# Unread matmuls between TensorE's steps at both ends of a lane-parallel recurrence

## The chip, the cores and the metric

One core of a Trainium2 chip runs the whole program. The metric is the device time of one execution in microseconds. TensorE (PE) does the matmuls, VectorE (DVE), ScalarE (ACT) and GpSimd (POOL) work on their results. A difference of about 0.2%, 6 us here, is what a measurement of this kernel can tell from no change.

## The reference

Two blocks of a language model run one after the other. The first begins with an RWKV-7 time mix over 528 tokens (16 meta tokens and 512 of the sequence), 16 heads of 64. The part in question is its recurrence, once for each head:

```python
def step(S, inp):
    r_t, w_t, k_t, v_t, a_t, b_t = inp
    sa = jnp.einsum('bhij,bhj->bhi', S, a_t)
    S = (S * w_t[:, :, None, :] + sa[..., None] * b_t[:, :, None, :]
         + v_t[..., None] * k_t[:, :, None, :])
    return S, jnp.einsum('bhij,bhj->bhi', S, r_t)
...
_, y = lax.scan(step, S0, seq)
y = jnp.moveaxis(y, 0, 1)
...
return (y * g) @ w_o, v_first
```

Everything after it (norm, gate, output matrix, a convolutional feed-forward network, attention, and the second block with ten times the work) is the same in both kernels.

## The kernel before

The recurrence is not run token by token. The 528 tokens are cut into chunks c = 0 to 3 of 128 tokens and a last chunk c = 4 of 16, and inside a chunk the recurrence is solved with matmuls: a triangular inverse is built by doubling. Two heads make a block (`blk`, 0 to 7), which the code also calls a lane, and two lanes make a couple (`pr`, 0 to 3). A couple goes through a fixed list of steps for each chunk (`lane_steps`): `g0` and `g1` (products within the chunk, the states' decay folded in), `x1`, then `W` and `X` by turns for each level of the doubling (six levels in a chunk of 128, three in the last), then `s1`, `s2`, `s3` and `y`. That makes 19 steps for each of the first four chunks and 13 for the last, 89 in all.

Each step is a few matmuls on PE, followed by the copy or the masking of their result out of PSUM on another engine (`scan_act`, `scan_dve`, `scan_pool`), which the couple's next step waits for. `g0` to `x1` hang on DVE (masks) and POOL, `W` to `X` on a DVE multiplication by a mask, `X` to the next `W` on an ACT copy, `y` to the next chunk's `g0` on POOL and DVE (the new state St).

The order is written out by hand in `SCAN`: in round t, couple p does its step t - 5p (`SKEW` is 5). So couple 0 is alone in rounds 0 to 4, couples 0 and 1 in rounds 5 to 9, three in rounds 10 to 14, four in rounds 15 to 88, then couples 1 to 3 in rounds 89 to 93, couples 2 and 3 in 94 to 98, and couple 3 alone in 99 to 103. All engines follow this one order, and PE executes its steps strictly in it. Each couple has its own two banks of PSUM (bank number = lane number).

Ahead of the recurrence stand the projections (`proj_pe`, line 912) with small sums of line 891; the first `g0` waits for DVE's copy of these sums (`p_sb`, line 1161). Behind it stands `gate_pe`: pairs of `mean(k)` (line 1463) and `squares(k)` (line 1472), which wait for the last `c_ye`, ACT's copy of the last `y`. On ACT and DVE the first work behind the recurrence is the split of a weight chunk (line 296, then 303), and only then DVE's centring of the first piece (line 1559) and ACT's squares (line 1540).

`ident` and `ones` are constants of 128 x 128 in f32, in the tile `cst`. The PE helper lines in the recurrence: 1269 (`g0`, `g1`), 1280, 1283 and 1286 (`x1`), 1295 (`W`), 1302 and 1305 (`X`), 1313 (`s1`), 1319 (`s2`), 1326 to 1329 (`s3`), 1335 to 1350 (`y`). In the profile an f32 matmul has two records for one in the program, an f16 one has one.

Of the kernel before, what the change touches and what calls it, by code (L numbers as in the profile page):

```python
# [7 lines left out]
F32 = mybir.dt.float32  # L8
# [230 lines left out]
def program(nc, d_h, d_ctx, d_vec, d_cst, d_csr, d_csb, d_csw, d_slc, d_w, d_ada, d_cond, d_out):  # L239
    with ExitStack() as ctx:  # L240
# [10 lines left out]
        psum = ctx.enter_context(nc.psum_tensor("psum", [128, 8, 512], F32))  # L251
# [6 lines left out]
        ident = cst[:, CST["ident"]:CST["ident"] + 128]  # L258
        ones = cst[:, CST["ones"]:CST["ones"] + 128]
# [402 lines left out]
        RA = mem.left("RA", [128, 2, 8, L])  # L662
# [4 lines left out]
        KT = mem.left("KT", [128, 8, L])  # L667
# [17 lines left out]
        BT = mem.left("BT", [128, 8, L])  # L685
        vtok = mem.left("vtok", [128, 5, D])
# [13 lines left out]
        v_out = more(r_out, [(j, b) for j in range(4) for b in range(3)])  # L700
# [21 lines left out]
        p_sb = sig("p_sb", [(ti,) for ti in range(5)])  # L722
# [451 lines left out]
        IH = mem.left("IH", [128, 128], F16)  # L1174
# [15 lines left out]
        def lane_steps(c):  # L1190
            n = 7 if c < 4 else 4
            out = ["g0", "g1", "x1"]
            for lvl in range(1, n):
# [5 lines left out]
        _steps = [(c, s) for c in range(5) for s in lane_steps(c)]  # L1199
        SCAN = [(p, *_steps[_t - SKEW * p]) for _t in range(len(_steps) + 3 * SKEW) for p in range(4)  # L1200
                if 0 <= _t - SKEW * p < len(_steps)]
        ONES = [(blk, c, s) for p, c, s in SCAN for blk in (2 * p, 2 * p + 1)]
        at = lambda name: [(blk, c) for blk, c, s in ONES if s == name]
        lvls = lambda name: [(blk, c, s[1] if s[0] == "X" else 0) for blk, c, s in ONES if s[0] == name or (name == "X" and s == "x1")]
# [45 lines left out]
        mUI = csr[:, CSR["mUI"]:CSR["mUI"] + 128]  # L1250
        lvT0 = csr[:, CSR["lvT0"]:CSR["lvT0"] + 128]

        def scan_pe(e):
            for pr, c, s in SCAN:
                two = [Lane(blk, c) for blk in (2 * pr, 2 * pr + 1)]
                if s in ("g0", "g1"):
                    w = int(s[1])
                    if w:
                        e.wait_ge(*c_gm.at(two[1].blk, c, 0, 1))
                    elif c:  # L1260
                        e.wait_ge(*c_S.at(two[1].blk, c - 1, 1))
                    else:
                        e.wait_ge(*p_sb.at(4))
                        e.wait_ge(*p_op.at("r", two[1].blk))
                        e.wait_ge(*v_out.at(3, 2))
                    for l, q in enumerate(two):
                        for j in range(2):
                            rows = slice(64 * j, 64 * j + 64)
                            ins = e.matmul(q.pg[:, j, l, :, 0:q.T], (BT, KT)[w][rows, q.blk, q.tok], RA[rows, :, q.blk, q.tok],  # L1269
                                           start=True, stop=True)  # L1270
                    ins.then_inc(*c_g.up(pr, c, w))
                    continue
                for q in two:
                    blk, T = q.blk, q.T
                    if s == "x1":
                        e.wait_ge(*c_ai.at(blk, c, 1))
                        e.wait_ge(*c_gm.at(two[1].blk, c, 1, 1))
                        e.wait_ge(*c_I.at(1))
                        for j in range(2):
                            e.matmul(q.px[:, j, 0:T], q.Xh[0:T, 2 + j, 0:T], IH[0:T, 0:T], start=True, stop=True)  # L1280
                        if not c:
                            e.wait_ge(*c_S0.at(blk))
                        e.matmul(q.p[:, 256:384], RA[:, 0, blk, q.tok], q.S[:, :], start=True, stop=False, skip_group_check=True)
                        for j in range(2):
                            h = 2 * blk + j
                            ins = e.matmul(q.p[:, 256 + 64 * j:320 + 64 * j], q.Ak[0:T, j, 0:T], vtok[0:T, c, 64 * h:64 * h + 64],  # L1286
                                           start=False, stop=True, skip_group_check=True)
                        ins.then_inc(*c_x.up(blk, c, 0))
                    elif s[0] == "W":
                        e.wait_ge(*c_xe.at(blk, c, s[1] - 1))  # L1290
                        if s[1] == 1:
                            e.wait_ge(*c_ar.at(blk, c))
                            e.wait_ge(*c_z1e.at(blk, c))
                        for j in range(2):
                            ins = e.matmul(q.px[:, j, 0:T], q.Ah[0:T, j, 0:T], q.Xh[0:T, j, 0:T], start=True, stop=True)
                        ins.then_inc(*c_w.up(blk, c, s[1]))
                    elif s[0] == "X":
                        e.wait_ge(*c_we.at(blk, c, s[1]))
                        f = True
                        for j in range(2):  # L1300
                            if s[1] < q.NL - 1:
                                e.matmul(q.px[:, j, 0:T], q.Xh[0:T, 2 + j, 0:T], q.Wh[0:T, j, 0:T], start=f, stop=False,
                                         skip_group_check=True)
                                f = False
                            ins = e.matmul(q.px[:, 2 + j, 0:T], q.Wh[0:T, j, 0:T], q.Xh[0:T, 2 + j, 0:T], start=f, stop=True,  # L1305
                                           skip_group_check=True)
                            f = False
                        ins.then_inc(*c_x.up(blk, c, s[1]))
                    elif s == "s1":
                        e.wait_ge(*c_xe.at(blk, c, q.NL - 1))  # L1310
                        e.wait_ge(*c_zr.at(blk, c))
                        for j in range(2):
                            ins = e.matmul(q.p[:, 64 * j:64 * j + 64], q.X[0:T, j, 0:T], q.Zr[0:T, 64 * j:64 * j + 64],
                                           start=True, stop=True)
                        ins.then_inc(*c_s1.up(blk, c))
                    elif s == "s2":
                        e.wait_ge(*c_s1e.at(blk, c))
                        for j in range(2):
                            ins = e.matmul(q.p[:, 128 + 64 * j:192 + 64 * j], q.A[0:T, j, 0:T], q.Wr[0:T, 0, 64 * j:64 * j + 64].bitcast(F32),  # L1319
                                           start=True, stop=True)  # L1320
                        ins.then_inc(*c_s2.up(blk, c))
                    elif s == "s3":
                        e.wait_ge(*c_s2e.at(blk, c))
                        if c < 4:
                            for w, src in enumerate((BT, KT)):
                                e.transpose(q.p[:, 128 + 128 * w:256 + 128 * w], src[:, blk, q.tok], ident)
                        e.matmul(q.p[:, 0:128], II[0:T, 0:T], q.Wr[0:T, 0, :], start=True, stop=False, skip_group_check=True)
                        for j in range(2):
                            ins = e.matmul(q.p[:, 64 * j:64 * j + 64], q.X[0:T, j, 0:T], q.Wr[0:T, 1, 64 * j:64 * j + 64],
                                           start=False, stop=True, skip_group_check=True)  # L1330
                        ins.then_inc(*c_s3.up(blk, c))
                    elif s == "y":
                        y, st = q.pf[:, 128:128 + T], q.pf[:, 256:320]
                        e.wait_ge(*c_u.at(blk, c))
                        e.matmul(y, q.S[:, :], RA[:, 1, blk, q.tok], start=True, stop=False, skip_group_check=True)
                        for j in range(2):
                            h = 2 * blk + j
                            e.matmul(y[64 * j:64 * j + 64, :], vtok[0:T, c, 64 * h:64 * h + 64], q.R[0:T, 2 + j, 0:T],
                                     start=False, stop=False, skip_group_check=True)
                        if c < 4:  # L1340
                            for j in range(2):
                                h = 2 * blk + j
                                e.matmul(st[64 * j:64 * j + 64, :], q.tB[0:T, 1, 64 * j:64 * j + 64], vtok[0:T, c, 64 * h:64 * h + 64],
                                         start=False, stop=False, skip_group_check=True)
                        for j in range(2):
                            ins = e.matmul(y[64 * j:64 * j + 64, :], q.U[0:T, 64 * j:64 * j + 64], q.R[0:T, j, 0:T],
                                           start=False, stop=True, skip_group_check=True)
                        if c < 4:
                            for j in range(2):
                                ins = e.matmul(st[64 * j:64 * j + 64, :], q.tB[0:T, 0, 64 * j:64 * j + 64], q.U[0:T, 64 * j:64 * j + 64],  # L1350
                                               start=False, stop=True, skip_group_check=True)
                        ins.then_inc(*c_y.up(blk, c))

        def scan_act(e):
            e.wait_ge(*p_sb.at(4))
# [1825 lines left out]
```

## Time and profile before

| | us |
|---|---|
| median of 3 runs | 2995.22 |
| lowest, highest | 2992.68, 2999.0 |
| the profiled execution | 2993.15 |
| its span, first to last instruction | 2991.4 |
| the recurrence in it (first g0 to the gate's first matmul) | 276.9 |

The profile page divides the span into 40 slices of 75 us. The recurrence fills from the end of slice 4 to the end of slice 7. Views of single stretches give for each the busy time of every engine and the TensorE clock granted there (1.00 is 2.4 GHz, 0.50 is 1.2 GHz). Start times of PE are those of the first of a group of records; since matmuls are pipelined and their ends are modelled, the cost of one is better read from the distance between starts, or from the chain of waits, than from a record's duration.

### The profile page before, as it was taken

To read this page: it belongs to the slowest core of one execution; us is meant where nothing else is said; L and a number is where in the kernel's file an instruction comes from. 1 tells how busy PE (TensorE), PEld (TensorE's weight loads), DVE (VectorE), ACT (ScalarE), POOL (GpSimd) and SP (SyncE) were. 2 spreads that over 40 slices of the span, in tenths; PEclk is the share of its full clock that TensorE was granted. 3 is DMA by queue.
4 is the path that set the end of the run, shared out by engine and by line. 5 is a ranking of instruction groups with operands and counts; after the bars stand their busy time and mean duration, and the time that the engine had idled before them with its cause. 6 is when DMAs were issued, how large, how long until landed. Compare 5 with 4: busy or idle time off the path is not lost.

```text
span 2991.4 us, 46812 instructions
## 1 busy us (share of the span) xinstructions
PE 2913.9 (97%) x19658; PEld 2583.3 (86%) x19658; DVE 1797.0 (60%) x2666; ACT 1300.3 (43%) x2153; POOL 483.1 (16%) x405
## 2 busy tenths in 40 slices
PE   6998999999999999999999999999999999999999
PEld 6997887899999999999999977667888878788887
DVE  7776664579597453547949757655535543465453
ACT  4575664344243455644424445654323332343231
POOL 0002221123032000002303313001202111121020
PEclk9998997999999999999999999999999999999999
DMA  2210000245554321025545520102232222223232
GB/s 103 89 53 36 2 2 6 75 156 183 170 170 164 113 88 36 1 79 183 176 164 189 188 99 29 43 17 83 94 97 88 97 90 93 91 85 101 90 97 86
DMA packets 79554, 284.34 MB, mean 95 GB/s; under 512 B 8528, under 2 KB 9296, under 8 KB 78576
## 3 DMA queue, kind: packets, MB, share of 16 engines
q1 hardware_dynamic: 79344, 281.35, 28.1%
q8 instruction: 155, 2.54, 0.3%
q14 instruction: 55, 0.45, 0.0%
HBM read 274.96 MB, written 6.36 MB: 94 GB/s over the span
## 4 chain that ended last, share of the span: by engine, by line
PE 93%; DVE 4%; ACT 2%; issue 1%; POOL 1%; DMA 0%; SPq 0%; DVEq 0%; ACTq 0%
PE psum L348 67%; PE psum L2733 2%; PE psum L1893 2%; PE psum L912 2%; PE psum L2104 2%; PE psum L2086 1%; PE psum L2077 1%; PE psum L1269 1%; PE psum L848 1%; PE psum L539 1%; PE psum L1319 1%; PE psum L1286 1%; PE psum L2430 1%; PE psum L2727 1%; PE psum L2721 1%
## 5 line engine op out<-in xcount | busy, mean ns | idle before, releaser
L303 DVE TENSOR_TENSOR wlo<-wraw,whi 128x1024 fp32r<-128x1024 f32 (+2 forms) x398 | 507.7, 1297 | 614.7 <-ACT whi L296 605.8
L296 ACT CAST whi<-wraw 128x1024 fp32r<-128x1024 f32 (+2 forms) x398 | 396.3, 1021 | 495.2 <-PE psum L348 460.6
L431 DVE CUSTOM_DVE_ANT_0 araw<-araw,cond 128x1024 f32<-128x1024 f32 x112 | 181.1, 1654 | 0.0
L348 PE MATMUL psum<-f0xh,whi 128*128 128x264 f32 x704 | 143.1, 285 | 0.0
L348 PE MATMUL psum<-f0xh,wlo 128*128 128x264 f32 x704 | 143.0, 285 | 0.0
L348 PE MATMUL psum<-f0xl,whi 128*128 128x264 f32 x704 | 142.4, 284 | 0.0
L348 PE MATMUL psum<-f1xh,whi 128*128 128x258 f32 x704 | 141.9, 283 | 0.0
L348 PE MATMUL psum<-f1xh,wlo 128*128 128x258 f32 x704 | 141.9, 283 | 0.0
L348 PE MATMUL psum<-f1xl,whi 128*128 128x258 f32 x704 | 141.4, 282 | 0.0
L348 PE MATMUL psum<-f2xh,whi 128*128 128x512 f32 x352 | 139.1, 395 | 1.0 <-DVE f2xl L592 1.0
L348 PE MATMUL psum<-f3xh,whi 128*128 128x512 f32 x352 | 139.1, 395 | 1.0 <-DVE f3xl L592 1.0
L348 PE MATMUL psum<-f2xh,wlo 128*128 128x512 f32 x352 | 139.0, 395 | 0.0
L348 PE MATMUL psum<-f3xh,wlo 128*128 128x512 f32 x352 | 139.0, 395 | 0.0
L348 PE MATMUL psum<-f2xl,whi 128*128 128x512 f32 x352 | 139.0, 395 | 0.0
L348 PE MATMUL psum<-f3xl,whi 128*128 128x512 f32 x352 | 139.0, 395 | 0.0
L348 PEld LDWEIGHTS psum<-f0xh,whi 128*128 128x128 f32 x704 | 109.3, 189 | 0.1
L348 PEld LDWEIGHTS psum<-f1xh,wlo 128*128 128x128 f32 x704 | 109.2, 190 | 0.0
L348 PEld LDWEIGHTS psum<-f1xh,whi 128*128 128x128 f32 x704 | 109.1, 189 | 0.1
L348 PEld LDWEIGHTS psum<-f0xh,wlo 128*128 128x128 f32 x704 | 109.1, 189 | 0.0
L348 PEld LDWEIGHTS psum<-f1xl,whi 128*128 128x128 f32 x704 | 109.0, 189 | 0.0
L348 PEld LDWEIGHTS psum<-f0xl,whi 128*128 128x128 f32 x704 | 108.8, 188 | 0.0
L1371 ACT ACTIVATE XH<-psum 128x512 f16<-128x512 f32 (+1 forms) x176 | 88.6, 562 | 25.1 <-PE psum L1305 24.9
(515 smaller groups left out, 8193.9 us busy)
## 6 DMA issues: line engine op xcount, KB each, us to landing
wraw<-d_w SPq DMA_DIRECT2D x357, 512.0 KB, 3.4
araw<-d_ada SPq DMA_DIRECT2D x112, 512.0 KB, 3.3
wraw<-d_w SPq DMA_DIRECT2D x32, 384.0 KB, 3.6
hn<-d_h SPq DMA_DIRECT2D x4, 528.0 KB, 7.9
hres<-d_h SPq DMA_DIRECT2D x1, 2112.0 KB, 8.2
spill<-hres SPq DMA_DIRECT2D x1, 2112.0 KB, 7.4
hres<-spill SPq DMA_DIRECT2D x1, 2112.0 KB, 8.5
cond<-d_cond SPq DMA_DIRECT2D x2, 1024.0 KB, 4.8
```

The source lines that it names most:

```text
L296: e.copy(whi[0:rows, n % NH, 0:kt * cols], wraw[0:rows, n % NR, 0:kt * cols]).then_inc(*w_hi.up(n))
L303: e.tensor_tensor(wlo[0:rows, n % NH, 0:kt * cols], wraw[0:rows, n % NR, 0:kt * cols], whi[0:rows, n % NH, 0:kt * cols].bitcast(F32), ALU. ...
L348: ins = e.matmul(psum[0:bw, b0 + nb * len(sl) + si, 0:ln], l_ if z == 2 else h_, (xp.lo if z == 1 else xp.hi)[:, k, o:o + ln], start=k == ...
L431: e.tensor_tensor_reduce(out=w, in0=w, in1=self.c[:, col, :], scale=1.0, scalar=0.0, op0=ALU.mult, op1=ALU.add, accum_out=ada[:, ly, blk, ...
L539: ins = e.matmul(rms_psum(ntok, bank, h), ones, sq[:, i, h * half:(h + 1) * half], start=i == 0, stop=i == 2)
L848: ins = e.matmul(psum[:, key_bank(j) + 2 * nb + si, 0:ln], (wl if z == 2 else wh)[:, i, 128 * nb:128 * nb + 128], (xs.lo if z == 1 else xs ...
L912: ins = e.matmul(psum[0:ln, b, 256 * (ti % 2):256 * (ti % 2) + 256], a_, w_[:, i, :], start=k == 0 and z == 0 and ti % 2 == 0, stop=k == 7 ...
L1269: ins = e.matmul(q.pg[:, j, l, :, 0:q.T], (BT, KT)[w][rows, q.blk, q.tok], RA[rows, :, q.blk, q.tok], start=True, stop=True)
L1371: e.activation(to, q.px[:, o:4, 0:T], ACT.Copy).then_inc(*c_xe.up(blk, c, s[1]))
L1893: ins = e.matmul(psum[0:ln, b, 256 * (ti % 2):256 * (ti % 2) + 256], a_, w_[:, k - k0, :], start=k == 0 and z == 0 and ti % 2 == 0, stop=k ...
L2104: ins = e.matmul(psum[:, 6 + half, lo_ - a0:hi_ - a0], vz, wtt[:, w % 2, col + lo_ - a:col + hi_ - a], start=kb == 2 and hh % 2 == 0, stop ...
L2733: ins = e.matmul(psum[:, b, :], vw[:, ts_[q][0], kv, :], Pw[:, n % NP, :], start=q == 0, stop=q == NQ[g] - 1, skip_group_check=True)
```

## The change

Between PE's steps the kernel now issues matmuls whose result nobody reads, in the rounds in which fewer than four couples are under way. The function `unread` issues 2 x (4 - active) f32 matmuls of `ident` (stationary) with `ones` (moving, 128 columns), each complete in itself, after the last couple's step of the round: 6 a round while one couple is there, 4 with two, 2 with three. `LAST_IN` holds, for the last step of each round, the number of couples done and the number under way. While couples are still to start, the results go to bank 7 of PSUM, that of the last lane. When couples are done, they go to bank 0, and PE waits first for ACT's copy of couple 0's last `y` (`c_ye` of lane 1), whose bank it was. The rounds are 0 to 14 and 89 to 103: 5 x (6 + 4 + 2) = 60 matmuls on each side, 120 in all. Nothing else is changed: the body of `scan_pe` became `scan_step` and lost an indentation, so that line numbers behind it are 17 higher.

```diff
+        LAST_IN = {}
+        for _t in range(len(_steps) + 3 * SKEW):
+            there = [p for p in range(4) if 0 <= _t - SKEW * p < len(_steps)]
+            LAST_IN[(there[-1], *_steps[_t - SKEW * there[-1]])] = (there[0], len(there))
...
+        def unread(e, done, active):
+
+            if done:
+                e.wait_ge(*c_ye.at(1, 4))
+            for _ in range(2 * (4 - active)):
+                e.matmul(psum[:, 0 if done else 7, 0:128], ident, ones, start=True, stop=True)
+
         def scan_pe(e):
             for pr, c, s in SCAN:
-                two = [Lane(blk, c) for blk in (2 * pr, 2 * pr + 1)]
...
+                scan_step(e, pr, c, s)
+                done, active = LAST_IN.get((pr, c, s), (0, 4))
+                if active < 4:
+                    unread(e, done, active)
+
+        def scan_step(e, pr, c, s):
+            two = [Lane(blk, c) for blk in (2 * pr, 2 * pr + 1)]
...
```

PE's order at the start of the recurrence, rounds 0 to 3 (couple 0: g0, g1, x1, W). Line 891 is the last of the projections; before:

```order
L891 MATMUL psum<-cst,kqr 16x2
L1269 MATMUL psum<-RA,BT 128x256 x4
L1269 MATMUL psum<-RA,KT 128x256 x4
L1280 MATMUL psum<-IH,XH 128x128 x2
L1283 MATMUL psum<-St,RA 128x128
L1286 MATMUL psum<-vtok,AK 128x64 x2
L1280 MATMUL psum<-IH,XH 128x128 x2
L1283 MATMUL psum<-St,RA 128x128
L1286 MATMUL psum<-vtok,AK 128x64 x2
L1295 MATMUL psum<-XH,AH 128x128 x4
L1302 MATMUL psum<-WH,XH 128x128
```

The same place in the changed kernel (lines 17 higher; the unread matmuls are those of line 1262):

```order
L891 MATMUL psum<-cst,kqr 16x2
L1286 MATMUL psum<-RA,BT 128x256 x4
L1262 MATMUL psum<-cst 128x128 x6
L1286 MATMUL psum<-RA,KT 128x256 x4
L1262 MATMUL psum<-cst 128x128 x6
L1297 MATMUL psum<-IH,XH 128x128 x2
L1300 MATMUL psum<-St,RA 128x128
L1303 MATMUL psum<-vtok,AK 128x64 x2
L1297 MATMUL psum<-IH,XH 128x128 x2
L1300 MATMUL psum<-St,RA 128x128
L1303 MATMUL psum<-vtok,AK 128x64 x2
L1262 MATMUL psum<-cst 128x128 x6
```

No step has changed its place; six matmuls stand in front of each of the next steps.

PE's order at the end, rounds 99 to 103 (couple 3 alone, chunk of 16 tokens: X, s1, s2, s3, y) and the gate's first matmul; before:

```order
L1305 MATMUL psum<-XH,WH 16x16 x4
L1313 MATMUL psum<-Zr,XT 16x64 x4
L1319 MATMUL psum<-WR,ZA 16x64 x4
L1327 MATMUL psum<-WR,II 16x128
...
L1329 MATMUL psum<-WR,XT 16x64 x2
L1335 MATMUL psum<-RA,St 128x16
...
L1346 MATMUL psum<-RBK,ZA 64x16 x2
L1463 MATMUL psum<-RA,cst 128x264 x4
```

The same place in the changed kernel:

```order
L1322 MATMUL psum<-XH,WH 16x16 x4
L1262 MATMUL psum<-cst 128x128 x6
L1330 MATMUL psum<-Zr,XT 16x64 x4
L1262 MATMUL psum<-cst 128x128 x6
L1336 MATMUL psum<-WR,ZA 16x64 x4
L1262 MATMUL psum<-cst 128x128 x6
L1344 MATMUL psum<-WR,II 16x128
...
L1346 MATMUL psum<-WR,XT 16x64 x2
L1262 MATMUL psum<-cst 128x128 x6
...
L1363 MATMUL psum<-RBK,ZA 64x16 x2
L1262 MATMUL psum<-cst 128x128 x6
L1480 MATMUL psum<-RA,cst 128x264 x4
```

Here too the steps stand as before, with six matmuls ahead of s1, s2, s3 and y, and six more between the last y and the gate's first matmul.

## Rows read from the trace of the kernel before

**Rows 1.** The page: share of each engine, then the granted clock in 40 slices
```profile
PE 2913.9 (97%) x19658; PEld 2583.3 (86%) x19658; DVE 1797.0 (60%) x2666; ACT 1300.3 (43%) x2153; POOL 483.1 (16%) x405
PEclk9998997999999999999999999999999999999999
```

**Rows 2.** Busy time by stretch of 1 us: start of the recurrence
```profile
core 0: us, PE busy (x) PEld busy (x) DVE busy (x) ACT busy (x) POOL busy (x), PEclk, DMA share, GB/s
244.00:245.00 1.00, 0.54 (x2) 0.50 (x4) 0.40 (x5) 0.50 (x2) 0.00 (x0) 0.59 0.99 401
...
261.00:262.00 1.00, 0.36 (x5) 0.14 (x4) 0.80 (x4) 1.00 (x3) 0.92 (x2) 0.88 0.00 0
...
268.00:269.00 1.00, 0.87 (x11) 0.53 (x9) 0.50 (x2) 1.00 (x4) 0.00 (x0) 0.97 0.00 0
```

**Rows 3.** The same view at the end of the recurrence and behind it
```profile
489.00:490.00 1.00, 1.00 (x15) 0.95 (x14) 0.29 (x3) 0.70 (x4) 0.25 (x1) 0.97 0.00 0
490.00:491.00 1.00, 1.00 (x16) 0.92 (x16) 0.00 (x0) 0.19 (x2) 0.00 (x0) 0.50 0.00 0
...
527.00:528.00 1.00, 1.00 (x5) 0.83 (x4) 0.13 (x1) 0.00 (x0) 0.00 (x0) 0.76 0.96 414
```

**Rows 4.** PE in order of time: start, length, line, tiles, idle before
```profile
244.46 2.08 PE L1269 MATMUL psum<-RA,BT 64*128 64x256 f32 x8 [0.58 <-DVE sbt L1161]
248.14 2.08 PE L1269 MATMUL psum<-RA,KT 64*128 64x256 f32 x8 [1.60 <-DVE RBK L1397]
...
251.95 0.74 PE L1283 MATMUL psum<-St,RA 128*128 128x128 f32 x2
252.48 0.95 PE L1286 MATMUL psum<-vtok,AK 128*128 128x64 f32 x4
...
257.15 0.40 PE L1295 MATMUL psum<-XH,AH 128*128 128x128 f16 x2
```

**Rows 5.** The same, in rounds 10 to 16 of the start, at full clock
```profile
276.61 0.27 PE L1280 MATMUL psum<-IH,XH 128*128 128x128 f16 x2 [0.79 <-POOL XH L1422]
...
278.17 0.39 PE L1295 MATMUL psum<-XH,AH 128*128 128x128 f16 x4
...
280.50 0.61 PE L1313 MATMUL psum<-Zr,XT 128*128 128x64 f32 x4
...
287.55 0.44 PE L1283 MATMUL psum<-St,RA 128*128 128x128 f32 x2
287.82 0.56 PE L1286 MATMUL psum<-vtok,AK 128*128 128x64 f32 x4
```

**Rows 6.** The same, at the end: last full-clock y of 16 tokens, then rounds 90 on
```profile
489.17 0.38 PE L1335 MATMUL psum<-RA,St 128*128 128x16 f32 x2
...
489.81 0.52 PE L1335 MATMUL psum<-RA,St 128*128 128x16 f32 x2
...
497.47 0.39 PE L1313 MATMUL psum<-Zr,XT 16*16 16x64 f32 x4
...
503.95 0.40 PE L1269 MATMUL psum<-RA,BT 64*16 64x32 f32 x8 [0.35 <-DVE St L1412]
...
509.86 0.29 PE L1305 MATMUL psum<-XH,WH 16*16 16x16 f16 x4
...
516.00 0.43 PE L1305 MATMUL psum<-XH,WH 16*16 16x16 f16 x4 [0.22 <-DVE WH L1401]
```

**Rows 7.** The chain of waits through the last y and the gate's start
```profile
518.91 0.54 PE psum L1335 x2
...
521.36 3.89 PE psum L1463 x8
...
528.24 0.89 PE psum L1472 x4
```

**Rows 8.** DVE in order of time behind the last y
```profile
522.27 1.23 DVE L303 TENSOR_TENSOR wlo<-wraw,whi 128x1024 fp32r<-128x1024 f32 x1 [3.81 <-ACT whi L296]
523.53 0.71 DVE L1559 SCALAR_TENSOR_TENSOR RA<-psum,RA 128x528 f32<-128x528 f32 x1
```

More of the change, by code:

```diff
@@ L1251, in program @@
         lvT0 = csr[:, CSR["lvT0"]:CSR["lvT0"] + 128]
+        def unread(e, done, active):
[3 more added lines that the diff above has]
+                e.matmul(psum[:, 0 if done else 7, 0:128], ident, ones, start=True, stop=True)
         def scan_pe(e):
             for pr, c, s in SCAN:
-                two = [Lane(blk, c) for blk in (2 * pr, 2 * pr + 1)]
[L1256 to L1283, printed above, removed]
+                scan_step(e, pr, c, s)
@@ new lines, in scan_pe @@
+                done, active = LAST_IN.get((pr, c, s), (0, 4))
[3 more added lines that the diff above has]
+            two = [Lane(blk, c) for blk in (2 * pr, 2 * pr + 1)]
+            if s in ("g0", "g1"):
+                w = int(s[1])
+                if w:
+                    e.wait_ge(*c_gm.at(two[1].blk, c, 0, 1))
+                elif c:
+                    e.wait_ge(*c_S.at(two[1].blk, c - 1, 1))
+                else:
+                    e.wait_ge(*p_sb.at(4))
+                    e.wait_ge(*p_op.at("r", two[1].blk))
+                    e.wait_ge(*v_out.at(3, 2))
+                for l, q in enumerate(two):
+                    for j in range(2):
+                        rows = slice(64 * j, 64 * j + 64)
+                        ins = e.matmul(q.pg[:, j, l, :, 0:q.T], (BT, KT)[w][rows, q.blk, q.tok], RA[rows, :, q.blk, q.tok],
+                                       start=True, stop=True)
+                ins.then_inc(*c_g.up(pr, c, w))
+                return
+            for q in two:
+                blk, T = q.blk, q.T
+                if s == "x1":
+                    e.wait_ge(*c_ai.at(blk, c, 1))
+                    e.wait_ge(*c_gm.at(two[1].blk, c, 1, 1))
+                    e.wait_ge(*c_I.at(1))
+                    for j in range(2):
+                        e.matmul(q.px[:, j, 0:T], q.Xh[0:T, 2 + j, 0:T], IH[0:T, 0:T], start=True, stop=True)
+                    if not c:
+                        e.wait_ge(*c_S0.at(blk))
+                    e.matmul(q.p[:, 256:384], RA[:, 0, blk, q.tok], q.S[:, :], start=True, stop=False, skip_group_check=True)
+                    for j in range(2):
+                        h = 2 * blk + j
+                        ins = e.matmul(q.p[:, 256 + 64 * j:320 + 64 * j], q.Ak[0:T, j, 0:T], vtok[0:T, c, 64 * h:64 * h + 64],
+                                       start=False, stop=True, skip_group_check=True)
+                    ins.then_inc(*c_x.up(blk, c, 0))
+                elif s[0] == "W":
+                    e.wait_ge(*c_xe.at(blk, c, s[1] - 1))
+                    if s[1] == 1:
+                        e.wait_ge(*c_ar.at(blk, c))
+                        e.wait_ge(*c_z1e.at(blk, c))
+                    for j in range(2):
+                        ins = e.matmul(q.px[:, j, 0:T], q.Ah[0:T, j, 0:T], q.Xh[0:T, j, 0:T], start=True, stop=True)
+                    ins.then_inc(*c_w.up(blk, c, s[1]))
+                elif s[0] == "X":
+                    e.wait_ge(*c_we.at(blk, c, s[1]))
+                    f = True
+                    for j in range(2):
+                        if s[1] < q.NL - 1:
+                            e.matmul(q.px[:, j, 0:T], q.Xh[0:T, 2 + j, 0:T], q.Wh[0:T, j, 0:T], start=f, stop=False,
+                                     skip_group_check=True)
+                            f = False
+                        ins = e.matmul(q.px[:, 2 + j, 0:T], q.Wh[0:T, j, 0:T], q.Xh[0:T, 2 + j, 0:T], start=f, stop=True,
+                                       skip_group_check=True)
+                        f = False
+                    ins.then_inc(*c_x.up(blk, c, s[1]))
+                elif s == "s1":
+                    e.wait_ge(*c_xe.at(blk, c, q.NL - 1))
+                    e.wait_ge(*c_zr.at(blk, c))
+                    for j in range(2):
+                        ins = e.matmul(q.p[:, 64 * j:64 * j + 64], q.X[0:T, j, 0:T], q.Zr[0:T, 64 * j:64 * j + 64],
+                                       start=True, stop=True)
+                    ins.then_inc(*c_s1.up(blk, c))
+                elif s == "s2":
+                    e.wait_ge(*c_s1e.at(blk, c))
+                    for j in range(2):
+                        ins = e.matmul(q.p[:, 128 + 64 * j:192 + 64 * j], q.A[0:T, j, 0:T], q.Wr[0:T, 0, 64 * j:64 * j + 64].bitcast(F32),
+                                       start=True, stop=True)
+                    ins.then_inc(*c_s2.up(blk, c))
+                elif s == "s3":
+                    e.wait_ge(*c_s2e.at(blk, c))
+                    if c < 4:
+                        for w, src in enumerate((BT, KT)):
+                            e.transpose(q.p[:, 128 + 128 * w:256 + 128 * w], src[:, blk, q.tok], ident)
+                    e.matmul(q.p[:, 0:128], II[0:T, 0:T], q.Wr[0:T, 0, :], start=True, stop=False, skip_group_check=True)
+                    for j in range(2):
+                        ins = e.matmul(q.p[:, 64 * j:64 * j + 64], q.X[0:T, j, 0:T], q.Wr[0:T, 1, 64 * j:64 * j + 64],
+                                       start=False, stop=True, skip_group_check=True)
+                    ins.then_inc(*c_s3.up(blk, c))
+                elif s == "y":
+                    y, st = q.pf[:, 128:128 + T], q.pf[:, 256:320]
+                    e.wait_ge(*c_u.at(blk, c))
+                    e.matmul(y, q.S[:, :], RA[:, 1, blk, q.tok], start=True, stop=False, skip_group_check=True)
+                    for j in range(2):
+                        h = 2 * blk + j
+                        e.matmul(y[64 * j:64 * j + 64, :], vtok[0:T, c, 64 * h:64 * h + 64], q.R[0:T, 2 + j, 0:T],
+                                 start=False, stop=False, skip_group_check=True)
+                    if c < 4:
@@ L1284, in scan_pe @@
                         for j in range(2):
                             h = 2 * blk + j
-                            ins = e.matmul(q.p[:, 256 + 64 * j:320 + 64 * j], q.Ak[0:T, j, 0:T], vtok[0:T, c, 64 * h:64 * h + 64],
-                                           start=False, stop=True, skip_group_check=True)
[L1288 to L1352, printed above, removed]
@@ new lines, in scan_step @@
+                            e.matmul(st[64 * j:64 * j + 64, :], q.tB[0:T, 1, 64 * j:64 * j + 64], vtok[0:T, c, 64 * h:64 * h + 64],
+                                     start=False, stop=False, skip_group_check=True)
+                    for j in range(2):
+                        ins = e.matmul(y[64 * j:64 * j + 64, :], q.U[0:T, 64 * j:64 * j + 64], q.R[0:T, j, 0:T],
+                                       start=False, stop=True, skip_group_check=True)
+                    if c < 4:
+                        for j in range(2):
+                            ins = e.matmul(st[64 * j:64 * j + 64, :], q.tB[0:T, 0, 64 * j:64 * j + 64], q.U[0:T, 64 * j:64 * j + 64],
+                                           start=False, stop=True, skip_group_check=True)
@@ L1354, in scan_act @@
+                    ins.then_inc(*c_y.up(blk, c))
         def scan_act(e):
```

## The prediction

> **What bounds the kernel now.** I read the page first: PE is busy for 97% of the span and no other engine for more than 60% [rows 1], so anything added on PE has a price unless it falls into one of PE's gaps. The granted clock by slices is 0.9 or more but for two slices, the fourth with an 8 and the seventh with a 7 [rows 1]. Both touch an end of the recurrence, and that is where the change adds its matmuls, so the next view is the busy time by stretches of 1 us there. At the start the clock falls to its half level (1.2 GHz) at about 244.2, is full (2.4 GHz) from 261.1 for some 3.5 us, half again and full for good from 268.0 [rows 2]. Before the fall PE had done sums of two columns each for 2 us; before the rises it had been busy without a gap. At the end the clock falls at 489.97 and comes back only at 527.5, after six microseconds of the gate's long matmuls [rows 3]. So two stretches of 20 and 37.5 us run at half the clock, and these are all that the unread matmuls could win back. How much of such a stretch is tied to the clock differs: a step waits for DVE, ACT or POOL as often as for PE at the start [rows 4], and hardly at the end, where PE shows no gap over 0.4 us [rows 6].
>
> **What one unread matmul costs.** The nearest row is line 1283, one f32 matmul of 128 columns: its two records and the next line's start are 0.53 us apart at half clock (251.95 to 252.48) and 0.27 at full (287.55 to 287.82) [rows 4, 5]. A lower bound comes from long matmuls standing back to back, where loading weights is wholly hidden: four records of 264 columns in 0.89 us at full clock, eight in 3.89 at half [rows 7]; by columns that is 2 x 0.2225 x 128/264 = 0.22 us and 2 x 0.486 x 128/264 = 0.47. Unread matmuls stand in runs of 2 to 6, between the two kinds, so I take 0.24 and 0.48. A run of six is 1.44 or 2.88 us, of four 0.96 or 1.92, of two 0.48 or 0.96. All 120 together are 28.8 us at full clock, 57.6 at half, before anything is hidden.
> The Trainium skill ("TensorE: Matmul & The Clock Gate", "Step-by-step: what each phase is for") says that the engine pulls the loading of weights ahead of matmuls in flight; by it the lower bound would hold, and the sum would be up to 120 x 0.02 = 2.4 us smaller. Line 1283 costs more than that in this trace, but between matmuls of other types.
>
> **The start, rounds 0 to 14** (244.46 to 280.50, 36.0 us). PE's order is strict, so a run of unread matmuls delays the next step by what exceeds the gap there.
> Rounds 0 to 4: before, 12.7 us (244.46 to 257.15) [rows 4]. Round 0 begins at half clock: g0 2.08 and six unread 2.88 are 4.96 against 3.68, +1.3. PE has then no gap from 244.46 on, and I expect the full clock during round 0 or round 1. Round 1: g1 takes 1.1 to 2.1, and DVE's masks behind it (as the idle of 1.60 behind g0 [rows 4]) cover the six: 2.6 to 3.6 against 3.64. Round 2: x1 at full clock is 1.56 (276.61 to 278.17 [rows 5]), with six 3.0, against 2.94. Rounds 3 and 4, W and X of one couple: 0.25 and 0.43 of work at full clock and 1.44 each, 3.6 against 2.43. Sum 14.2 to 15.2, that is +1.5 to +2.5.
> Rounds 5 to 9 (257.15 to 269.84, 12.7 us): at full clock throughout 2.3 + 2.7 + 3.1 + 1.65 + 1.65 = 11.4, since g0, g1 and x1 halve and rounds 6 and 7 have waits for DVE under which the four unread lie: -1.3.
> Rounds 10 to 12 wait for masks too (0.79 us ahead of 276.61, and two like it), which covers 0.48: +0.1. Rounds 13 and 14 (278.17 to 280.50 [rows 5]) have no gap: +1.0.
> Start: **+1.8**, between 0 (0.22 each, clock back at once) and +3.5 (0.27, clock back in round 2).
>
> **Rounds 15 to 88** hold no added instruction; they start later and last as long. The clock's fall at 489.97 lies in round 88, while the first unread matmul of the end stands behind round 89's s3 (497.4). So the fall stays, and the first 7.4 us at half clock too. The wait for c_ye of lane 1 costs nothing: that y was finished at 490.8, and behind the wait only work of round 90 is queued.
>
> **The end, rounds 89 to 103 and the gate.** Work of T = 16 costs 0.6 at full clock of what it costs at half: the first lane's y is 0.64 us (489.17 to 489.81 [rows 6]), and 1.09 at half (the last y's first lane, 518.91 to 520.00, [rows 7] for its start).
> Rounds 89 to 93 (to 509.86): 5 x 0.96 = 4.8 at half clock, less 0.35 of the gap ahead of 503.95 [rows 6] and 0.15 of smaller ones: +4.3. Two in each round leave most of the time to matmuls of 16 rows or columns, under which the clock was not given back in 30 us although PE shows as busy, so I leave it at half here.
> Rounds 94 to 98 (509.86 to 516.00, 6.1 us [rows 6]): four unread fill two thirds of a round. I let round 94 pass at half (0.85 + 1.92 = 2.8) and the others at full clock: 3.1 of work and 4 x 0.96 = 7.0. Sum 9.8, **+3.6**.
> Rounds 99 to 103: to the last y's end before 5.1 us; after, 2.6 of work at full clock and 4 x 1.44 = 8.4, +3.3. The six behind the last y are hidden: DVE centres the first piece only at 523.53, after ACT's 1.04 and its own 1.23 on a weight chunk [rows 8], 2.4 us after y's end, and six unread plus mean(0) at full clock are 1.44 + 0.89 = 2.3. Behind that the gate gains from the clock what lies between 523.5 and 527.5: sixteen records of which DVE's and ACT's pieces set part, 1.4 us. Together **+1.9**.
> End: 4.3 + 3.6 + 1.9 = **+9.8**.
>
> **Sum.** 1.8 + 9.8 = +11.6 us on the profiled execution's 2993.15: 3004.8, taken as 3005. That execution lies 2.1 us under the median; the runs spread by 6.3, so I add nothing for it. Nothing behind the gate can swallow the shift, since PE is the bound there to the end [rows 1].
>
> **Rivals.**
> (a) The clock comes back early at the end, in round 90: couple 3's y of 128 tokens is 4.4 us of dense f32, followed now by unread ones. Then rounds 89 and 90 add 1.4, rounds 91 to 93 go from 7.4 to 4.6 + 1.4 = 6.0 (-1.4), rounds 94 to 98 need 3.4 + 4.8 = 8.2 (+2.1), and the last part stays +1.9: +4.0, with the start +5.8, 2999. For it: dense f32 preceded the rise at 527.5. Against it: the same y in 498.1 to 502.5 did not bring the clock back. This is **not slower** by my bound, and it decides at the point where the clock is full before 503.
> (b) It doesn't come back until the gate: +4.3; rounds 94 to 98 9.6 less 0.5 of gaps, +9.1; four runs of six 11.5 less 0.4, +11.1; the last run delays mean(0) past 523.5, +1.5. End +26, 3021. For it: PE shows 1.00 busy at half clock for 30 us [rows 3]. Against it: from round 99 on three quarters of PE's time would be full 128 x 128 f32 work. The Trainium skill ("TensorE: Matmul & The Clock Gate", "What's actually happening") says that the throttled state is the default and activity releases it. By it (a) or my forecast would hold rather than (b); the trace agrees at 261 and 527, and shows at 490 that a PE busy in the records isn't enough.
> (c) The start stays at half clock until 261 as before: rounds 0 to 4 then add 1.3 + 1.3 + 2.9 + 2.2 + 2.4 = 10.1, rounds 5 to 14 some 2, so the whole is +22, 3015.
> (d) Faster: the fall at 490 moves behind round 89, because the later start puts other rounds under the clock's look, and unread ones then hold it. That is worth 0.4 x 7.4 = 3 us on top of (a); with the start's best value of 0 the whole is +1 to -1, 2992 to 2994. So even this is no clear gain: 28.8 us of matmuls stand against stretches of 37.5 and 20 us at half clock, of which 0.4 at most, 15 and 8 us, could come back.
>
> **Chances.** My forecast 0.50, (a) 0.24, (b) 0.13, (c) 0.07, (d) 0.06. The range runs from (a) less 1.5 us to (b): 2997.5 to 3021. Measurement can tell 0.2% from no change. Slower by more (over 3001): forecast, (b), (c) and a part of (a), 0.73. Within: most of (a) and (d), 0.24. Faster: 0.03.
>
> **What the changed profile would show.** Half clock for under 8 us from 244, and round 15's s1 near 282; rounds 3 and 4 of 1.7 to 1.9 us, with six unread each; the fall in round 87 to 89 as before; the clock full again around round 95, and y's end to the gate's first matmul 1.5 us apart. I would be wrong in the sum if an unread matmul cost other than 0.22 to 0.27 us at full clock, and in the sign if the clock stayed full from round 88 on.

## The result, and the profile after

The changed kernel takes 3017.90 us (median of four runs, 3014.59 to 3024.2) against 2996.97 for the kernel before (four runs): 21 us more, a ratio of 1.0074 [1.0053, 1.0095]. The profiled execution took 3016.87, its span 3015.0 against 2991.4. Slower, as forecast, by more than the 11.6 us of the sum and inside the range. One execution of the kernel before in a later comparison took 4760 us at a mean granted clock of 0.553; it is left out of every figure here.

The page of the changed kernel: the engines' shares, then the granted clock by slices.

```profile
PE 2945.1 (98%) x19898; PEld 2616.7 (87%) x19898; DVE 1795.9 (60%) x2666; ACT 1300.5 (43%) x2153; POOL 483.7 (16%) x405
...
PEclk9999997999999999999999999999999999999999
```

PE has 240 records more (120 f32 matmuls, two records each) and 31.2 us more of busy time; the other engines are as in [rows 1]. The 8 in the fourth slice has gone, the 7 in the seventh has not. Stretches of 2 us of the changed kernel (columns as in [rows 2]; the last but two is the granted clock):

```profile
474.00:476.00 2.00, 1.66 (x34) 1.23 (x28) 2.00 (x13) 1.30 (x7) 0.70 (x4) 1.00 0.00 0
476.00:478.00 2.00, 2.00 (x22) 1.36 (x22) 0.95 (x9) 1.67 (x5) 0.23 (x1) 0.55 0.03 8
...
490.00:492.00 2.00, 1.39 (x28) 1.06 (x26) 1.15 (x5) 0.28 (x1) 0.60 (x1) 1.00 0.00 0
...
504.00:506.00 2.00, 2.00 (x19) 1.43 (x20) 0.00 (x0) 0.70 (x5) 0.00 (x0) 0.50 0.00 0
...
512.00:514.00 2.00, 2.00 (x38) 1.78 (x37) 0.53 (x5) 0.86 (x6) 0.78 (x4) 1.00 0.00 0
...
518.00:520.00 2.00, 2.00 (x19) 1.65 (x19) 0.00 (x0) 0.59 (x4) 0.00 (x0) 0.50 0.00 0
...
532.00:534.00 2.00, 2.00 (x10) 2.00 (x11) 0.00 (x0) 0.11 (x2) 0.00 (x0) 0.50 0.00 0
534.00:536.00 2.00, 2.00 (x19) 1.82 (x18) 0.00 (x0) 0.42 (x2) 0.00 (x0) 0.94 0.00 0
...
1188.00:1190.00 2.00, 2.00 (x11) 2.00 (x9) 1.46 (x3) 1.49 (x3) 0.00 (x0) 0.50 0.00 0
```

Followed us by us, the clock is at half in 244 to 247.5 (before: 17 + 3.4 us there [rows 2]), in 476 to 490, which the kernel before shows at full clock, in 493 to 510, in 517.2 to 534.2, and later for ten us in the attention (1186 to 1196) and for 3.4 us at 1773. PE in order of time at the two ends; line 1262 is the unread matmuls, 1480 the gate's first:

```profile
244.15 2.08 PE L1286 MATMUL psum<-RA,BT 64*128 64x256 f32 x8 [0.58 <-DVE sbt L1161]
246.16 2.23 PE L1262 MATMUL psum<-cst 128*128 128x128 f32 x12
248.33 1.14 PE L1286 MATMUL psum<-RA,KT 64*128 64x256 f32 x8
249.39 1.60 PE L1262 MATMUL psum<-cst 128*128 128x128 f32 x12
251.03 0.27 PE L1297 MATMUL psum<-IH,XH 128*128 128x128 f16 x2
...
252.59 1.56 PE L1262 MATMUL psum<-cst 128*128 128x128 f32 x12
253.98 0.39 PE L1312 MATMUL psum<-XH,AH 128*128 128x128 f16 x4
...
503.36 1.20 PE L1262 MATMUL psum<-cst 128*128 128x128 f32 x4
504.49 0.39 PE L1330 MATMUL psum<-Zr,XT 16*16 16x64 f32 x4
...
519.69 2.08 PE L1262 MATMUL psum<-cst 128*128 128x128 f32 x8
521.69 1.03 PE L1336 MATMUL psum<-WR,ZA 16*16 16x64 f32 x8
...
531.79 2.75 PE L1262 MATMUL psum<-cst 128*128 128x128 f32 x12
534.48 0.30 PE L1330 MATMUL psum<-Zr,XT 16*16 16x64 f32 x4
534.71 1.60 PE L1262 MATMUL psum<-cst 128*128 128x128 f32 x12
...
541.33 1.60 PE L1262 MATMUL psum<-cst 128*128 128x128 f32 x12
542.77 1.95 PE L1480 MATMUL psum<-RA,cst 128*128 128x264 f32 x8
```

Six cost 1.39 us at full clock (252.59 to 253.98), 0.23 each; four cost 2.0 at half (519.69 to 521.69), 0.50 each. The parts, each from one step's start to another's:

| part | before | after | difference |
|---|---|---|---|
| rounds 0 to 14 (first g0 to couple 0's first s1) | 36.0 | 35.8 | -0.2 |
| rounds 15 to 89 (to the last transpose of s3) | 216.1 | 222.7 | +6.5 |
| from there to the gate's first matmul | 24.7 | 40.1 | +15.4 |
| gate, to its second squares | 6.7 | 4.4 | -2.3 |
| everything behind (+4.5) and ahead (-0.3) | | | +4.2 |

### The profile page after: what moved, and what is told of

It is laid out like the page before. It is cut to its first block, busy times and chain, and to the rows that moved or that the text cites. A ratio compares the mean times of both kernels' runs of the same rounds, so it can differ in the third digit from the quotient of the medians.

```text
span 3015.0 us, 47292 instructions
## 1 busy us (share of the span) xinstructions
PE 2945.1 (98%) x19898; PEld 2616.7 (87%) x19898; DVE 1795.9 (60%) x2666; ACT 1300.5 (43%) x2153; POOL 483.7 (16%) x405
## 4 chain that ended last, share of the span: by engine, by line
PE 93%; DVE 4%; ACT 1%; issue 1%; POOL 0%; DMA 0%; SPq 0%; DVEq 0%; ACTq 0%
PE psum L348 67%; PE psum L2750 2%; PE psum L1910 2%; PE psum L912 2%; PE psum L2121 2%; PE psum L1262 1%; PE psum L2103 1%; PE psum L2094 1%; PE psum L1286 1%; PE psum L848 1%; PE psum L539 1%; PE psum L1336 1%; PE psum L2447 1%; PE psum L2744 1%; PE psum L2738 1%
```

## Experiments

One yardstick for all: the three stretches of the recurrence in one profiled execution, and the ratio to the kernel before where it was timed. "Early stretch" is half clock that begins between 460 and 480 us; it lies ahead of a fall between 485 and 495 that every profile has. "End to gate" begins at the last transpose of round 89.

| kernel | rounds 0-14 | 15-89 | end to gate | early stretch | ratio |
|---|---|---|---|---|---|
| before | 36.0 | 216.1 | 24.7 | no | |
| before, profiled again | 34.7 | 223.6 | 24.7 | 460-477 | |
| the change | 35.8 | 222.7 | 40.1 | 476-490 | 1.0074 [1.0053, 1.0095] |
| start only | 35.8 | 222.7 | 24.7 | 474-488 | 1.0002 [0.9991, 1.0013] |
| end only | 34.7 | 223.6 | 42.8 | 463-480 | 1.0058 [1.0037, 1.0078] |
| 12 behind round 14 | 38.6 | 221.9 | 24.2 | 478-491 | 1.0020 [1.0009, 1.0031] |
| rounds 0 to 2 only | 32.4 | 222.8 | 24.7 | 470-485 | 0.9992 [0.9979, 1.0004] |
| the same, timed again | 32.4 | 222.9 | 24.7 | 473-487 | 0.9985 [0.9974, 0.9996] |
| end only, doubled | 36.5 | 221.3 | 46.5 | 479-489 | |
| end only, f16 | 35.4 | 216.0 | 33.0 | no | |
| f16, both ends | 34.2 | 217.1 | 33.1 | no | 1.0051 [1.0032, 1.0071] |
| hold, f32 | 32.4 | 222.0 | 27.2 | no | 1.0004 [0.9994, 1.0013] |
| hold, f16 | 32.2 | 219.3 | 26.4 | no | 1.0012 [1.0000, 1.0024] |

**Which side costs: start only, end only.** (The words behind # in the edits shown here are notes for the reader.)

```diff
-                if active < 4:
+                if active < 4 and not done:      # start only
+                if active < 4 and done:          # end only
```

> Unread matmuls in rounds 0 to 14 alone (60 of them), none at the end. Theory A (the lost time is the price of unread matmuls at the end; the stretch of half clock at 476 to 489.5 is a matter of where the clock's changes fall, not of the unread matmuls themselves): rounds 0 to 14 take 35.8 us as in the changed kernel, and the whole is within 6 us of the kernel before, on either side. Theory B (the start's matmuls move the recurrence so that the clock falls near 476 each time, which costs some 6.5 us): half clock shows before round 86 again and the kernel is 6 us or more slower than before. The forecast's sum had +1.8 us for the start.

> Unread matmuls in rounds 89 to 103 alone. Theory A: rounds 89 to 103 take 38 to 42 us against 26.2 before, the gate gives back 2, so the kernel is 12 to 15 us slower than before, and the rounds before 89 are as in the kernel before. Theory B: the same end, and the fall of the clock at 490 as before, so 12 to 15 too; start only and end only would then add up to the change's 21. If the clock stays full from round 90 on (the second rival of the prediction), only 4 us slower.

Start only is the same as before (1.0002), end only 17 us slower (1.0058, 11 to 23). So the end's 60 matmuls account for nearly all of the change's loss. End only lost more than the 12 to 15 expected: in its profile the clock was at half again from 514.4 to 538.3. And end only, whose program is the kernel before up to round 89, had the early stretch (462 to 464 at 0.80, 468 at half). So it isn't the start's shift that brings it (theory B): that fell here.

**A shift alone: 12 unread matmuls behind round 14.**

```diff
+                if t == 14:
+                    unread(e, 0, -2)
```

> The kernel before with one run of 12 unread matmuls behind round 14, at full clock: rounds 15 to 103 are the same work, only shifted by 12 x 0.23 = 2.8 us. Theory A: 2.8 us for the run; where the clock falls in rounds 75 to 90 changes with the shift, so the total lies anywhere from 0 to 9 us above before. Theory B, as far as it blames the shift: half clock before round 86 shows here also. If the clock falls in round 88 as in the kernel before, the shift alone doesn't move the fall.

The twelve stand in one run (line 1262), ahead of round 15's s1 (line 1330):

```profile
276.75 0.54 PE L1322 MATMUL psum<-XH,WH 128*128 128x128 f16 x4
...
278.10 2.90 PE L1262 MATMUL psum<-cst 128*128 128x128 f32 x24
280.75 0.61 PE L1330 MATMUL psum<-Zr,XT 128*128 128x64 f32 x4
```

Round 14 with them lasts from 276.75 to 280.75, 4.0 us, where the two profiles of the kernel before have 1.3: 2.7 us for the twelve, as their price says. The whole is 6 us slower (1.0020, 3 to 9). That is more than 2.7 by its median, and its lower end agrees with 2.7; what the rest is, if it is anything, no stretch of this profile shows. The early stretch is there once more, as theory A allows and theory B asks.

**Is the early stretch the kernel's own: before, profiled again.**

> The kernel before, unchanged, profiled once more. In five profiles of kernels with unread matmuls (one of which has none ahead of round 89) the clock fell between 463 and 477, came back for some 3 to 12 us near 481 to 494 and fell again; rounds 15 to 89 took 222 to 224 us there, and 216 in the one profile of the kernel before. Theory A (that stretch comes and goes on its own and was absent from the first profile by chance): half clock shows near 460 to 480 here too, and round 15's s1 to round 89's last transpose takes about 222. Theory B (it comes from the unread matmuls or the new program): it is absent again, 216.

Stretches of the kernel before in this second profile:

```profile
456.00:458.00 2.00, 1.44 (x26) 1.10 (x26) 1.30 (x6) 1.36 (x3) 0.60 (x1) 1.00 0.00 0
...
462.00:464.00 2.00, 2.00 (x15) 1.10 (x13) 0.24 (x1) 0.34 (x2) 0.00 (x0) 0.50 0.03 8
...
468.00:470.00 2.00, 2.00 (x16) 2.00 (x16) 0.00 (x0) 1.04 (x3) 0.00 (x0) 0.50 0.00 0
...
476.00:478.00 2.00, 1.82 (x27) 1.31 (x26) 1.78 (x9) 1.47 (x3) 0.12 (x1) 0.68 0.00 0
...
480.00:482.00 2.00, 2.00 (x21) 1.44 (x21) 0.54 (x5) 1.35 (x6) 0.00 (x0) 1.00 0.03 8
```

The unchanged kernel has it, with 223.6 us for rounds 15 to 89. It comes up in the rounds in which the 16-token chunk's small matmuls begin to replace large ones, and it comes and goes from one execution to another: of the profiles without any addition between rounds 15 and 88, eight have it and three have not (before, f16 end, f16 both ends). So the +6.5 in the table of parts is no cost of the change. The first profile of the kernel before, on which the prediction was built, happened to lack it. The granted clock of whole executions says the same: that profile had 0.987, and of the 64 later runs of the kernel before 46 had 0.982 to 0.985.

**Does the clock follow the number or the kind: doubled, f16.** Both on top of end only.

```diff
-            for _ in range(2 * (4 - active)):
+            for _ in range(4 * (4 - active)):      # doubled
...
+            for _ in range(8 * (4 - active)):      # f16
+                e.matmul(psum[:, 0 if done else 7, 0:128], IH[:, :], IH[:, :], start=True, stop=True)
```

> Unread matmuls at the end alone, twice as many (4, 8 and 12 a round, 120 in all). By price alone at full clock 60 more cost 60 x 0.23 = 13.8 us over the end-only kernel's 42.8 from round 89's last transpose to the gate: 57. Theory C (in rounds 94 to 98 the clock stayed at half because the unread matmuls were too few beside work of 16 columns): with eight a round it is full from round 94 or 95 on, rounds 94 to 98 take 13 us or less in spite of 20 more matmuls (14.8 in the changed kernel), and the whole end is 50 to 52. Theory D (the clock follows something else there): half clock in rounds 94 to 98 again, these alone 25 us, the end 60 or more.

> Unread matmuls at the end alone, in f16 (the f16 identity with itself, 128 columns), four for each f32 one: 8, 16 and 24 a round. One f16 matmul stands 0.055 us from the next at full clock and 0.107 at half in this trace, so four cost 0.22 or 0.43 us, as one f32. Theory C: the end takes as long as with f32, 38 to 43 us, with the clock full or half in much the same rounds. If f16 ones at the same time of PE bring the clock back in rounds 94 to 98 where f32 ones did not, the end takes about 33 to 35: then the kind of matmul matters and not only PE's busy time.

Doubled (rounds 91, then 95 and 96), then f16 (rounds 94 to 98); the unread matmuls are those of line 1262:

```profile
511.71 1.16 PE L1262 MATMUL psum<-cst 128*128 128x128 f32 x8
512.80 0.23 PE L1344 MATMUL psum<-WR,II 16*16 16x128 f32 x1
...
521.26 2.05 PE L1262 MATMUL psum<-cst 128*128 128x128 f32 x16
523.24 0.61 PE L1336 MATMUL psum<-WR,ZA 16*16 16x64 f32 x8
...
523.87 2.05 PE L1262 MATMUL psum<-cst 128*128 128x128 f32 x16
```

```profile
509.27 1.79 PE L1262 MATMUL psum<-IH 128*128 128x128 f16 x16
511.00 0.39 PE L1330 MATMUL psum<-Zr,XT 16*16 16x64 f32 x4
...
511.60 1.63 PE L1262 MATMUL psum<-IH 128*128 128x128 f16 x16
513.16 0.62 PE L1336 MATMUL psum<-WR,ZA 16*16 16x64 f32 x8
...
513.79 1.07 PE L1262 MATMUL psum<-IH 128*128 128x128 f16 x16
...
515.41 1.07 PE L1262 MATMUL psum<-IH 128*128 128x128 f16 x16
```

Eight f32 unread matmuls take 1.98 us at full clock here (521.26 to 523.24), as long as four at half in the changed kernel: twice as many cost nothing more in these rounds, because the clock was full. The doubled end took 46.5 us, 3.7 more than end only, where 60 matmuls at full clock cost 13.8. Both forecasts for the end, 50 to 52 and 60 or more, were too high. Of the two, theory C is the one that this profile bears out: more unread work held the clock. It doesn't say how much is needed in a round. After its rise at 510 the doubled kernel's clock did not fall again in the recurrence, neither in rounds 91 to 93, where four stood beside the matmuls of 16 columns, nor in rounds 94 to 98 with eight. In the changed kernel two a round stood in rounds 91 to 93; the clock fell just behind them, at 517.2, and four a round did not bring it back in 17 us. So four a round held a full clock in one place and didn't restore it in another, and it is one profile of the doubled kernel.

With f16 the clock rose at 503, fell for 3.4 us at 509.5 and was full from 513 on; the end took 33.0. The rise is no earlier in the work than with f32: 7.3 us behind the last transpose, against 7.7 to 8.1 in the profiles of the change, of end only and of the doubled kernel. What differs is the fall behind it, 3.4 us long instead of 17 and 24.

**The change with f16.**

> The change itself with f16 instead of f32, four for one, so that PE's time for them is the same (480 instead of 120). Theory E (f16 matmuls of the same length bring the clock back sooner): the end takes 33 us from round 89's last transpose to the gate, as with the end alone in f16, against 40.2 with f32; with 2.3 back in the gate and 35 to 36 at the start, 5 to 9 us slower than before where the change is 21 slower. Theory C (it was chance that the clock came back early in that one profile): 38 to 43 again, and 15 to 22 us slower than before.

The profile repeats the 33 at the end, but the runs don't repeat the profile: it took 3004.70 at a mean granted clock of 0.991, the other three 3013 to 3017 at 0.986 or 0.987, which is 24 to 30 us more at half clock. The ratio is 1.0051 [1.0032, 1.0071], and overlaps the change's. So the forecast of 5 to 9 us fell for the median. In two profiles out of two the second fall was shorter with f16 than in the two profiles with as much f32. But these are also the two that lack the early stretch, which both f32 ones have, so the kind of matmul isn't the only difference; an advantage over f32 isn't shown.

**What is worth keeping: rounds 0 to 2 alone.**

```diff
+                if 0 <= t < 3:
+                    unread(e, done, active)
```

> Six unread matmuls in each of rounds 0 to 2 only, 18 in all. In the changed kernel rounds 0 to 4 took 13.3 us with 30 unread matmuls, of which those of rounds 0 and 1 lay under masks on DVE and those of rounds 2 to 4 in the open. Theory A: the clock rises at 247.5 as in the changed kernel; if it then stays full without further unread matmuls, rounds 0 to 14 take 33 us or less against 36.0 before, and the kernel is 3 us faster than before, less than its runs spread. If the clock falls again at about 258 to 265, as it did there in the kernel before, the gain is 1 us or nothing.

> The kernel with six f32 unread matmuls in each of rounds 0 to 2 and none elsewhere, measured again with more rounds, since 0.9992 [0.9979, 1.0004] leaves open whether it is faster. Its profile had rounds 0 to 14 at 32.4 us, against 36.0 and 34.6 in the two profiles of the kernel before. If that holds, 2 to 3.6 us faster, a ratio of 0.9988 to 0.9993. If the clock's other changes swamp it, 1.0000.

PE in the second of these profiles:

```profile
246.75 2.14 PE L1262 MATMUL psum<-cst 128*128 128x128 f32 x12
248.82 1.13 PE L1286 MATMUL psum<-RA,KT 64*128 64x256 f32 x8
249.89 1.60 PE L1262 MATMUL psum<-cst 128*128 128x128 f32 x12
251.53 0.27 PE L1297 MATMUL psum<-IH,XH 128*128 128x128 f16 x2
...
253.09 1.56 PE L1262 MATMUL psum<-cst 128*128 128x128 f32 x12
...
257.06 1.13 PE L1286 MATMUL psum<-RA,BT 64*128 64x256 f32 x8
...
259.81 1.14 PE L1286 MATMUL psum<-RA,KT 64*128 64x256 f32 x8 [1.05 <-DVE RBK L1414]
...
262.51 0.27 PE L1297 MATMUL psum<-IH,XH 128*128 128x128 f16 x2 [1.24 <-POOL XH L1439]
```

The six of round 0 and the six of round 1 lie for the most part under the waits for DVE's masks, and g1's records take 1.13 instead of 2.08 [rows 4]: round 1 falls from 3.6 to 2.7 us. The six of round 2 lie in the open, but x1 beside them runs at full clock, and the round takes 2.9 us, as before. Behind them the clock stays full though PE has gaps again; rounds 3 to 14 take 3.2 us less than in the first profile of before and 1.8 less than in the second, which is most of the gain. Rounds 0 to 14 take 32.4 us in both profiles, against 36.0 and 34.7 before. Measured first, the kernel's difference was not clear of zero; measured again, it is 0.9985 [0.9974, 0.9996], some 4.5 us faster than before, anything from 1 to 8. The granted clock agrees: 20 of this kernel's 21 runs had 0.987 or more, of the kernel before's 64 only 11. So it is faster than both kernels, by somewhat less than 0.2%.

**Holding the clock through the last chunk: f32, f16.** Besides rounds 0 to 2, unread matmuls of 112 columns ahead of lane 0's own in couple 0's steps of the last chunk (rounds 76 to 88), and a few in rounds 89 to 93. The second kernel has f16 ones throughout, 24 a round in rounds 0 to 2.

```diff
+        def fill(e, q):
+            if q.blk == 0 and q.c == 4:
+                for _ in range(2):                 # 4, and IH twice, in the f16 kernel
+                    e.matmul(psum[:, 0, 400:512], ident, ones[:, 0:112], start=True, stop=True)
...
+                if 0 <= t < 3 or 89 <= t < 94:
+                    unread(e, done, active)
```

> Candidate. Six unread matmuls in rounds 0 to 2 as in the run of the first three rounds; two of 112 columns in each of couple 0's steps of the last chunk (rounds 76 to 88, ahead of its own matmuls, lane 0 only), two in rounds 89 to 93; none behind. The price at full clock is 18 + 26 to 44 + 10 times some 0.2. If these hold the clock from round 76 on, rounds 15 to 89 take 217 to 220 us instead of 222.8, rounds 89 to 93 about 12 instead of 14.8, and with the start's 2 to 3.6 us the kernel is 5 to 9 us faster than before. If the clock falls near 470 all the same, ahead of or in spite of them, they cost 8 to 15 us at half clock and the kernel is 4 to 12 us slower.

> Candidate with f16 unread matmuls: 24 in each of rounds 0 to 2 (as long as six f32 ones), four of 112 columns in each of couple 0's steps of the last chunk (rounds 76 to 88), four in rounds 89 to 93, none behind. In the hold with f32 ones the early stretch of half clock was absent but they cost 4 us at full clock, so nothing was won. Here the price is 13 x 4 x 0.05 = 2.6 us. If f16 ones hold the clock from 470 to 490 or beyond, rounds 15 to 89 take 218 to 219 us against 216 (no early stretch) and 223 (with it), and the whole is 3 to 7 us faster than before. If the clock falls near 488 as ever and stays down to the gate, 0 to 3 us faster; if it falls early too, 0 to 3 us slower.

Neither had the early stretch, but both fell to half at 486 all the same, the second for 41 us. Rounds 15 to 89 took 222.0 and 219.3 instead of the 216 to 217 of executions without the stretch: most of what the stretch costs went into the matmuls that were to prevent it, and neither the 5 to 9 us hoped for from the first kernel came nor the 0 to 7 from the second. With ratios of 1.0004 and 1.0012 both are 4 to 8 us worse than rounds 0 to 2 alone. Since the stretch also stays away by itself, two profiles don't show that they prevented it.

## Why the prediction was right, point by point

**The sign and its reason held.** PE is the bound, the clock's fall lies ahead of the end's first unread matmul, and their price at the end exceeds what the clock gives back. Start only and end only show this apart: 0 and 17 us.

**The price** of 0.24 and 0.48 a piece was 0.23 and 0.50.

**Start, forecast +1.8**: -0.2 against the profile it was reckoned from, +1.2 against the second one of the kernel before. The clock rose within round 0, which took 4.2 us (244.15 to 248.33) where 5.0 was reckoned for all of it at half clock. Rounds 1 and 2 came out as reckoned, 2.70 and 2.95 us (248.33 to 251.03 to 253.98).

**Rounds 15 to 88, forecast 0**: +6.5 in the profiles, not from the change. The text took one execution of the kernel before for the kernel: it said that the two stretches of 20 and 37.5 us were all there was at half clock, and these rounds have a third in most profiles.

**End, forecast +9.8**, +13.1 to the same place (the gate's second squares). The first part, rounds 89 to 93, was over-sized: 13.2 us before from the last transpose to round 94, 14.2 after, +1.0 instead of +4.3, since the clock did rise at 510.3, behind round 90's y, as rival (a) said. The failed term is the next: I let the clock be full from round 95 on, with 9.8 us for rounds 94 to 98. It fell at 517.2, in round 94, and stayed at half through all of them although PE shows 1.00 busy: 14.8 us, +8.6 instead of +3.6. That is rival (b)'s value for these rounds (+9.1). Rounds 99 to 103 to the end of the last y took 9.7 where 8.4 was reckoned, as their first run of six was still at half (2.75 us). The last six were hidden and the gate gained 1.1 from the last y's end, 1.4 forecast. The end's +9.8 thus came near +13.1 partly by luck: 3.3 too much in one part stood against 5.0 and 1.6 too little behind it.

**The rest.** +4.5 us of the profiled difference lie behind the gate. The changed kernel's profile has half clock there at 1186 to 1196, which neither profile of before has and that of f16 at both ends does. I take it for the executions' own spread (before: 2987.8 to 3004.0 over the runs of all comparisons); that the unread matmuls have no part in it isn't shown. Of the profiled +23.6, then, 13 us belong to the change (start -0.2, end +15.4, gate -2.3), and 15.5 by the second profile of before. The medians differ by 21, with an interval from 16 to 28, and the end-only kernel's by 17, from 11 to 23. A part of the 21 is the comparison's: the four runs of before in it have a median of 2996.97, the 64 of the later ones medians of 2998.4 to 2999.8, which would make it 18 to 20. The 3 to 7 us that remain are not traced to a stretch. The forecast of 3005 was too low by the term of rounds 94 to 98, and because it was added to one execution of the kernel before that had less half clock than most; that the result lay inside the range owes something to its width up to rival (b).

## What to carry to other kernels

Here unread matmuls paid only where they lay in waits that exist anyway and where the clock stayed up behind them by itself: 18 of the 120 were worth 4.5 us [1 to 8], and with the other 102 the kernel is some 25 us slower than with the 18 alone. In rounds where PE has no gap they are work like any other, and a stretch at half clock gives back some 0.4 of its length where PE is the bound (20 us more of it in rounds 15 to 89 cost 7.5 us in the second profile of before) and less where the steps wait for other engines. Before costing a change of a few us by the granted clock, profile the kernel before twice: in the two profiles here the stretches at half clock add up to 80 and 92 us.

## What was not expected of the hardware

A PE that is busy without a gap can stay at half clock: 17 us in the changed kernel (517.2 to 534.2), with four f32 matmuls of 128 x 128 and a step of 16-column matmuls by turns, at 1.00 busy. In the one profile of the doubled kernel the same place stayed at full clock with eight, so twice the unread work took the same 2 us. The Trainium skill ("TensorE: Matmul & The Clock Gate", "Why this matters for your kernels") advises to keep TensorE busy continuously to get past the throttle; these rows show that being busy by the records is not enough, since PE was busy throughout. The kernel before shows it less clearly: of the 28 us from 492 to 520, all at half clock, its PE was busy for 26.8.
